# Second layer's gated retention output: PE transposes replaced by VectorE block turns and two rounds of DMA through DRAM

## Reference

```python
def odd_mixer(u, w_in, w_out, onorm_g, cos_c, sin_c):
    qc, kc, vc, gc = jnp.split(u @ w_in, ODD_SPLITS, axis=-1)
    qh, kh = apply_rope(qc...), apply_rope(kc...)
    o = retention_chunkwise(qh, kh, vc.reshape(B, S, C_HEADS, C_DV))
    o = rmsnorm(o, onorm_g) * jax.nn.silu(gc.reshape(B, S, C_HEADS, C_DV).astype(jnp.float32))
    return o.reshape(B, S, C_VW).astype(u.dtype) @ w_out
```

## Time and profile before

| | |
|---|---|
| median of 3 runs | 1418.0 us (1417.61 to 1418.11) |
| the profiled execution | 1417.72 us, of which the profile's span is 1415.9 us |
| PE busy | 1400.1 us of the span |
| DVE, ACT, POOL busy | 967.6, 744.2, 75.1 us |
| DMA | 272.62 MB, mean 193 GB/s |

### The profile page before, as it was taken

How to read it: one execution, slowest core, us unless ns; L and a number is a source line. 1 busy time by engine, 2 the same in 40 slices (tenths; PEclk the granted TensorE clock), 3 DMA queues, 4 the chain that set the end, 5 groups by cost and what they waited for, 6 DMA issues and landing times.

```text
span 1415.9 us, 18299 instructions
## 1 busy us (share of the span) xinstructions
PE 1400.1 (99%) x7090; PEld 1188.8 (84%) x7090; DVE 967.6 (68%) x929; ACT 744.2 (53%) x792; POOL 75.1 (5%) x92
## 2 busy tenths in 40 slices
PE   7999999999999999999999999999999999999998
PEld 6888888888888888888888888888888888888887
DVE  6879796786775666776774686774774656677736
ACT  4674676545553557655553565553544445455534
POOL 0000000010000100110000010000202102000000
PEclk9999999999999999999999999999999999999999
DMA  9747454465555553464455474556453633645541
GB/s 393 305 150 273 175 190 163 167 240 209 181 184 203 197 197 119 149 212 175 178 194 225 160 270 152 201 183 234 164 222 119 219 138 144 228 178 178 209 178 45
DMA packets 40388, 272.62 MB, mean 193 GB/s; under 512 B 4609, under 2 KB 5505, under 8 KB 8706
## 3 DMA queue, kind: packets, MB, share of 16 engines
q1 hardware_dynamic: 36864, 261.65, 50.3%
q10 hardware_dynamic: 3458, 10.04, 2.2%
HBM read 270.62 MB, written 1.05 MB: 192 GB/s over the span
## 4 chain that ended last, share of the span: by engine, by line
PE 98%; DMA 1%; DVE 0%; SPq 0%; issue 0%; ACT 0%; DVEq 0%; POOLq 0%; POOL 0%; ACTq 0%
PE acc L2299 20%; PE acc L2300 20%; PE acc L2492 20%; PE acc L2500 10%; PE acc L2311 10%; PE acc L2337 10%; PE turn L2365 3%; DMA mod_raw<-in_units 1%; PE turn L2533 0%; PE aux L2440 0%; PE aux L2789 0%; PE aux L2293 0%; PE aux L2295 0%; PE aux L2294 0%; DVE mod_part L1424 0%; PE acc L2295 0%
## 5 line engine op out<-in xcount | busy, mean ns | idle before, releaser
L1305 DVE TENSOR_TENSOR wlo<-raw,whi 128x2048 fp32r<-128x2048 f32 x233 | 533.2, 2297 | 139.1 <-ACT whi L442 138.9
L442 ACT ACTIVATE whi<-raw 128x2048 fp32r<-128x2048 f32 x233 | 444.9, 1915 | 252.9 <-PE acc L2337 102.7
L2299 PE MATMUL acc<-whi,feeds 128*128 128x512 f32 x840 | 333.1, 397 | 0.0
L2300 PE MATMUL acc<-whi,feeds 128*128 128x512 f32 x840 | 326.2, 389 | 0.0
L2492 PE MATMUL acc<-feeds,whi 128*128 128x512 f32 x1216 | 292.9, 392 | 0.0
L2492 PEld LDWEIGHTS acc<-feeds,whi 128*128 128x128 f32 x1216 | 223.1, 188 | 43.5
L2299 PEld LDWEIGHTS acc<-whi,feeds 128*128 128x128 f32 x840 | 158.5, 189 | 34.1 <-issue 1.6
L2300 PEld LDWEIGHTS acc<-whi,feeds 128*128 128x128 f32 x840 | 158.6, 189 | 30.8 <-issue 0.2
L2311 PE MATMUL acc<-wlo,feeds 128*128 128x512 f32 x616 | 165.6, 391 | 0.0
L2500 PEld LDWEIGHTS acc<-feeds,wlo 128*128 128x128 f32 x1216 | 155.9, 191 | 6.0
L2500 PE MATMUL acc<-feeds,wlo 128*128 128x256 f32 x1216 | 157.7, 283 | 0.0
(11 more groups left out here) (378 smaller groups left out, 1238.0 us busy)
## 6 DMA issues: line engine op xcount, KB each, us to landing
raw<-in_units SPq DMA_DIRECT2D x237, 1024.0 KB, 4.8
mod_raw<-in_units SPq DMA_DIRECT2D x6, 1024.0 KB, 10.7
gpost<-in_norm_g ACTq DMA_DIRECT2D x8, 512.0 KB, 4.9
gpre<-in_norm_g ACTq DMA_DIRECT2D x6, 512.0 KB, 6.6
mod_more<-in_units SPq DMA_DIRECT2D x2, 1024.0 KB, 23.3
h<-in_x SPq DMA_DIRECT2D x2, 512.0 KB, 10.1
w_ax<-in_w_ax SPq DMA_DIRECT2D x1, 1024.0 KB, 26.4
bgate<-in_b_gate SPq DMA_DIRECT2D x1, 1024.0 KB, 27.7
```

What stands on the lines that cost most here:

```text
L442: act.activation(whi[:, u % RING, :], raw[:, u % RING, :], ACT.Copy).then_inc(hi_ready, 1)
L1305: dve.tensor_tensor(wlo[:, u % RING, :], raw[:, u % RING, :], whi[:, u % RING, :].bitcast(F32), ALU.subtract).then_inc(lo_ready, 1)
L2299: pe.matmul(out, xh, wh, start=first, stop=False)
L2300: pe.matmul(out, xl, wh, start=False, stop=False)
```

## The change

The 32 PE transposes go. In their place, for each piece k: DVE turns the 128 x 1024 piece in blocks of 32 x 32 right behind `gate_out(k)`, into `xn` (`out_blocks`, one instruction); ACT issues a store of the 512 KB into a DRAM scratch (`store_blocks`), waits until it has landed, and issues four loads of 128 KB that bring the blocks back to the right partitions (`load_blocks`), into `sgc`, in runs of 1 KB; then ACT rounds (`out_hi`) and DVE subtracts (`out_lo`) from `sgc` in place of the PSUM tile `turn`. `fed(k)` on PE waits for `out_lo(k)`.

```diff
@@ -100,7 +100,7 @@
 
 
 ODD_Q, ODD_K, ODD_G0, ODD_G1, ODD_V0, ODD_V1, ODD_O0, ODD_O1 = range(8)
-RET_TURNS, RET_MIXES = (43, 48, 52, 57), (38, 43, 48, 52)
+RET_STORES, RET_LOADS, RET_FEEDS, RET_MIXES = (42, 47, 51, 56), (44, 48, 52, 57), (46, 49, 53, 57), (38, 43, 48, 52)
 RET_SQUARES, RET_OUT = (39, 44, 48, 53), (41, 46, 50, 55)
 ODD_TURNS = {7: 0, 12: 1, 15: 0, 20: 1}
 ODD_HEADS = {23: (0, 1), 25: (2, 3)}
@@ -361,6 +361,8 @@
 
         v_ready = sem("v_ready")
         att_rounded, att_split, vc_rounded = sem("att_rounded"), sem("att_split"), sem("vc_rounded")
+        out_blocked, out_stored, out_turned = sem("out_blocked"), sem("out_stored"), sem("out_turned")
+        out_fed_hi, out_fed = sem("out_fed_hi"), sem("out_fed")
         ret_mixed, ret_taken = sem("ret_mixed"), sem("ret_taken")
         aux_ready, aux_read = sem("aux_ready"), sem("aux_read")
         f_sig, logs_ready, b_ready = sem("f_sig"), sem("logs_ready"), sem("b_ready")
@@ -404,6 +406,27 @@
         def wait_gate_used(engine, r):
 
             engine.wait_ge(mod_used, MODS_USED + r + 1)
+
+        turned_blocks = nc.dram_tensor("turned_blocks", (2 * TOK, P, D), F32, kind="Internal").ap()
+
+        def by_blocks(ap, b):
+
+            return ap.rearrange("p (c b i) -> p b c i", b=4, i=P // 4) if b is None else \
+                ap.rearrange("(a i) (b e) -> b i a e", a=4, b=4)[b]
+
+        def gated_out(k):
+
+            return sgc[:, k % TOK, 2 * (k // TOK):2 * (k // TOK) + 2, :].rearrange("p a d -> p (a d)")
+
+        def out_feeds(k, i):
+
+            def by_column(ap):
+                return ap.rearrange("p c (a j) -> p c a j", a=4)
+
+            hi_part, lo_part = (feed2_hi, feed2_lo) if k < TOK else (feed_hi, feed_lo)
+            part = (slice(None), slice(4 * i, 4 * i + 4), lanes(k % TOK))
+            src = gated_out(k).rearrange("p (a c j) -> p c a j", a=4, c=KC)[:, 4 * i:4 * i + 4]
+            return src, by_column(hi_part[part]), by_column(lo_part[part])
 
         def by_two(ap):
 
@@ -1090,20 +1113,40 @@
                     act.activation(xn[:, t, C_DV:], aux[:, 1, :], ACT.Square, accum_out=ssm[:, k, 1:2])\
                         .then_inc(sqm_ready, 1)
 
+                def store_blocks(k):
+
+                    act.wait_ge(out_blocked, k + 1)
+                    act.dma_start(turned_blocks[k], xn[:, k % TOK, :]).then_inc(out_stored, 16)
+
+                def load_blocks(k):
+
+                    act.wait_ge(out_stored, 16 * (k + 1))
+                    for b in range(4):
+                        act.dma_start(gated_out(k)[32 * b:32 * b + 32, :].rearrange("p (a e) -> p a e", a=4),
+                                      by_blocks(turned_blocks[k], b)).then_inc(out_turned, 16)
+
+                def out_hi(k):
+
+                    act.wait_ge(out_turned, 16 * 4 * (k + 1))
+                    for i in range(2):
+                        y, hi_part, _ = out_feeds(k, i)
+                        act.activation(hi_part, y, ACT.Copy).then_inc(out_fed_hi, 1)
+
                 for s in range(8 * ODD_O1 + 2):
                     g, j = s // 8, s % 8
-                    if s in RET_TURNS:
-                        k = RET_TURNS.index(s)
-                        if s % 8 == 0:
-                            evacuate(g - 1, 1)
-                        feed(feed2_hi if k < TOK else feed_hi, k % TOK)
-                    elif j == 0 and 1 <= g <= ODD_V1:
+                    if j == 0 and 1 <= g <= ODD_V1 + 1:
                         evacuate(g - 1, 1)
                     if s == 53:
                         hi()
                     if s in ATT_SPLITS:
                         for a in ATT_SPLITS[s]:
                             attention_hi(a)
+                    if s in RET_STORES:
+                        store_blocks(RET_STORES.index(s))
+                    if s in RET_LOADS:
+                        load_blocks(RET_LOADS.index(s))
+                    if s in RET_FEEDS:
+                        out_hi(RET_FEEDS.index(s))
                     if s in RET_SQUARES:
                         squares(RET_SQUARES.index(s))
                     if j == 4 and g <= ODD_V1:
@@ -2231,6 +2274,19 @@
                             settle()
                     ins.then_inc(ret_taken, 1)
 
+                def out_blocks(k):
+
+                    dve.wait_ge(ret_taken, k + 1)
+                    dve.transpose(xn[:, k % TOK, :].rearrange("p (b c i) -> p b c i", b=4, c=KC),
+                                  by_blocks(gated_out(k), None)).then_inc(out_blocked, 1)
+
+                def out_lo(k):
+
+                    for i in range(2):
+                        y, hi_part, lo_part = out_feeds(k, i)
+                        dve.wait_ge(out_fed_hi, 2 * k + i + 1)
+                        dve.tensor_tensor(lo_part, y, hi_part.bitcast(F32), ALU.subtract).then_inc(out_fed, 1)
+
                 for s in range(8 * ODD_O1 + 2):
                     g, j = s // 8, s % 8
                     if s in ODD_TURNS and j == 4:
@@ -2242,11 +2298,11 @@
                         no_sums(0)
                     elif j == 4 and g <= ODD_V1:
                         values_lo(g, 0)
-                    if s in RET_TURNS:
-                        k = RET_TURNS.index(s)
-                        feed(*((feed2_lo, feed2_hi) if k < TOK else (feed_lo, feed_hi)), k % TOK)
                     if s in RET_OUT:
                         gate_out(RET_OUT.index(s))
+                        out_blocks(RET_OUT.index(s))
+                    if s in RET_FEEDS:
+                        out_lo(RET_FEEDS.index(s))
                     if s in ODD_HEADS:
                         dve.wait_ge(odd_loaded, 16 * 2)
                         for a in ODD_HEADS[s]:
@@ -2920,20 +2976,12 @@
                                          vc_hi[:, c, a, :], vc_lo[:, c, e, :], c == 0, c == t)
                     last.then_inc(ret_mixed, 1)
 
-                def turned_out(k):
-
-                    pair, t = k // TOK, k % TOK
-                    pe.wait_ge(ret_taken, k + 1)
-                    uses[k] = n["tb"], n["tb"] + 1
-                    feed_rows(sgc[:, t, 2 * pair:2 * pair + 2, :].rearrange("p a d -> p (a d)"))
-
                 def fed(k):
 
-                    for use in uses[k]:
-                        pe.wait_ge(moved[use % 2], use // 2 + 1)
+                    pe.wait_ge(out_fed, 2 * (k + 1))
 
                 all_moved()
-                uses, u0, evacuated = {}, n["u"], list(n["e"])
+                u0, evacuated = n["u"], list(n["e"])
                 n["u"] += 8 * RING
                 for s in range(8 * (ODD_O1 + 1)):
                     g, t, i = s // 8, s // 4 % 2, s % 4
@@ -2950,8 +2998,6 @@
                         if ODD_HEADS[s][0] == 0:
                             all_moved()
                         scores(ODD_HEADS[s])
-                    if s in RET_TURNS:
-                        turned_out(RET_TURNS.index(s))
                     if s in RET_MIXES:
                         mix(RET_MIXES.index(s))
                     if i == 0 and g >= ODD_O0:
```

## The result

The changed kernel takes 1432.7 us (median of 4 runs, 1431.2 to 1435.4) against 1418.05 us (4 runs beside it): 14.7 us slower, ratio 1.0106, 95% interval [1.0095, 1.0118]. The forecast of 1416.3 us and its range up to 1422.5 us were both wrong. The profiled execution took 1431.24 us with a span of 1429.3; that of before 1417.72 and 1415.9.

A forecast was written before the change was run, and what follows sets the result against it. The prediction took PE's instruction list to bound the kernel: -3.5 us for transposes, +1.5 for slot 60, +0.3 for mix(3) and mix(1) make -1.7, so 1416.3 us against the 1418.0 median, range 1414.2 to 1422.5, chance 0.43.

The forecast's parts named there:

- What goes, and the turn: Four groups of eight PE transposes come off the path, -3.5 us; each DVE block turn takes 1.3 us, bounds 0.7 and 2.3.
- Store and loads undisturbed: A 512 KB store lands in 2.8 us; four 128 KB loads on ACT's queue take 3.8 us from first issue to landing.
- Pieces 0 and 2 are hidden: Piece 0 has 19 us to slot 48 against 10 needed; piece 2 has 4 us to spare at slot 56.
- the slack at slots 56 and 57: PE needs piece 2 at slot 56, 4 us to spare, and the rest of (7,1) in slot 57, 1.1 us to spare.
- Pieces 0 and 1: From gate_out(0) to slot 48 and gate_out(1) to slot 52: 19 and 16 us available against 10 us needed.
- 0.7 us to spare: Ahead of mix(3): gate_out(2), behind out_lo(1) on DVE, ends at 1160.8; PE comes at 1161.5.
- the term of 0.3 us for mix(3) and mix(1) together: Allowance of 0.3 us in the sum for PE waiting at gate_out(2) ahead of mix(3) and at mix(1).
- Piece 3: Its loads meet weight units, land 6.0 us after first issue; DVE feeds until 1187.3, PE stands at slot 60 at 1186.0.
- the term of 1.5 us for slot 60: PE's wait for piece 3's feeds, computed as 1.3 us and taken as 1.5; range 0 to 3.5 us.
- ACT's own rate of the earlier trace: 0.81 MB in 3 us on ACT's queue; gives piece 3's 512 KB 1.9 us behind a weight unit.
- the weight loads go first: Queues alternate packets, 1 KB against 7: slot 60 waits 5 to 6 us, mix(3) 1.5 late; 1421.5 us; chance 0.24.
- The clock: A 5 us wait at slot 60 drops PE to 1.2 GHz, +2.4 us more, 1424; counted in the weight-loads-first rival's 0.24.

The follow-up runs named there:

- without the rounds: Changed kernel with the DMA stores and loads left out, block turns and feeds from SBUF kept: 1414.7 us, 0.9976 of the kernel before.
- The run with 4 KB rows: Changed kernel, but the store moves the blocks in 1 KB runs and one DMA of 4 KB rows loads each piece: about 1423 us, ratio 1.0037.
- with the units held: Changed kernel, but SP holds back seven weight units beside the loads of pieces 1 and 3 until these have landed: 1419.8 us, ratio 1.0012.
- the run with copies: Changed kernel without the DMA stores and loads, plus twelve ACT copies ahead of piece 3's feeds, so PE waits without new DMA: 1423.2 us.

## Why the prediction was wrong

- *What goes, and the turn.* Right. -3.5 us (3.4 measured without the rounds); the turn, put at 1.3 us, takes 1.245:

```profile
L2280 DVE STREAM_TRANSPOSE xn<-sgc x4: 1245/1246/1246, 1132.8 to 1182.3; 128x1024 f32<-128x1024 f32 x4
```

- *Store and loads undisturbed.* Right: 2.6 us for 2.8, and some 4 us for 3.8 where the loads meet nothing (the last goes out 1.35 us behind the first, and each lands in 2.5 to 2.9). Each 256 KB more costs (4.8 - 2.1) / 3 = 0.9 us by its rows, not 0.8; that changes nothing. Pieces 0 and 2 are hidden as said, and the slack at slots 56 and 57 held.
- *Pieces 0 and 1.* This step failed first. The forecast saw the place that counts: out_lo(1) stands ahead of `gate_out(2)` on VectorE, so mix(3) waits for piece 1. But it gave piece 1 the undisturbed 3.8 us and set no weight unit beside its loads; they took 13.45. "0.7 us to spare" became 4.7 us of waiting, and the term of 0.3 us for mix(3) and mix(1) together should have been 4.7, with 1.6 more for the clock. The run with 4 KB rows marks the edge: 7.2 us were still in time.
- *Piece 3.* The second step that failed. The forecast let one unit pass first and landed the loads 6.0 us behind their first issue; it was 11.84, and the store took 3.9 in place of 2.8. These 5.8 and 1.1 us more make the term of 1.5 us for slot 60 into 8.4; it is 8.5. The step took ACT's own rate of the earlier trace rows for what follows the unit; that row had little beside it, and 1 KB packets beside units get the 0.04 MB in a us of the queue rows above.
- *The rival "the weight loads go first"* had the mechanism, the two places and the sign, with a chance of 0.24. Its sizes were too small: 1.5 us at mix(3) for 4.7, 5 to 6 at slot 60 for 8.5. It had reckoned piece 3's landing at about 10 us, and took piece 1's lateness without working it out. The queue rows at 512 B, 1 KB and 4 KB show 46 packets to 44, 40 to 44 and 33 to 32. The Trainium skill (DMA: Bandwidth & Descriptors, Queues, rings and completion order) says that an engine goes round the queues it has work for at packet granularity, and that a packet is typically 9 to 17 descriptors. The rows agree that the queues take turns, except for units that were queued first (last section); but what changes places here is one packet as the profile counts it, a single run of 512 B to 8 KB.
- *The clock.* Priced at 2.4 us for one wait of 5 us, in the rival only. Measured 2.6 with one wait of 6.1 us, and 1.6 behind each of the two in the changed kernel, 3.2 in sum.
- *What decided it* was the choice between the earlier trace rows. Both cases stood in the trace of before; the forecast took the row of the empty queue for a moment at which a unit is released every 2.2 us.

## What to carry to other kernels

A transfer's time belongs to the moment at which it runs: before moving work from an engine to DMA, list what is on the other queue then, and compare packet sizes, not bytes. Beside a stream of long packets, short ones cost about one long packet each (some 40 to 45 passed in a us here, of 512 B or of 1 KB). Put them into the same queue ahead of the stream, and look at what the displaced stream then meets. And where an engine works in order, the deadline of a late step is that of the step behind it: reckon slack to there.

## What the runs showed that had not been expected

A transfer that is issued behind a queued unit lets that unit pass whole before it takes turns: first packets 3 us after the issue for the loads of piece 1, against 0.5 to 1 us with the units held; the store behind four held units, 6.9 us to landing. It goes the other way too: the unit issued at 1150.69 moved its first packet after 1153.5, behind some 160 packets of the loads., on which the rival rested, is such a moment and no row of turns. The load of 7.8 us of the earlier trace rows went out with the unit, and from 1018 to 1019, in the kernel before, hardly a packet of it passed:

```profile
q1 hardware_dynamic: 51, 0.42, 99.4%
q10 hardware_dynamic: 1, 0.00, 1.0%
```

Whether such a start follows the order of issue or what the engines had already taken in was not tried.

The granted clock can fall after a wait as well as within it. In the stretches of the changed kernel (the column third from the end), PE idle from 1161.8 to 1166.5 and from 1192.8 to 1201.3:

```profile
1165.00:1166.00 1.00, 0.00 (x0) 0.00 (x0) 0.96 (x2) 0.00 (x0) 0.00 (x0) 1.00 0.04 8
1167.00:1168.00 1.00, 1.00 (x4) 0.71 (x3) 0.67 (x1) 0.00 (x0) 0.00 (x0) 0.50 0.00 0
1196.00:1197.00 1.00, 0.00 (x0) 0.00 (x0) 0.00 (x0) 0.00 (x0) 0.00 (x0) 1.00 1.10 397
1198.00:1199.00 1.00, 0.00 (x0) 0.00 (x0) 0.00 (x0) 0.00 (x0) 0.00 (x0) 0.50 0.11 30
1205.00:1206.00 1.00, 1.00 (x6) 0.82 (x5) 0.69 (x1) 0.10 (x1) 0.00 (x0) 1.00 0.00 0
```

Behind the 4.7 us wait the clock still reads 1.00 while PE idles and 0.50 once it works again; in the 8.5 us wait it falls midway, and part of the slow stretch passes in the idle time. So the short wait costs as much on top as the long one, 1.6 us; behind the wait of 6.1 us in the run with copies, where the clock read 0.50 through all of slot 60, it was 2.6.
